# A hybrid decoder layer on one core: transposed sample probabilities taken by matmul with a selection matrix, in place of transposes

## What is computed

```python
def dsa_sample(q, k, v, qi, wi, kidx, cache_k, cache_v, cache_kidx, page_table):
    ...
    sc = jnp.where(causal[None], indexer_scores(qi, wi, kidx_all), -jnp.inf)
    _, idx = lax.top_k(sc, topk)            # 256 of 2056 keys for each new token
    ...
    return sparse_core(q, k_sel, v_sel, valid)

def sparse_core(q, k_sel, v_sel, valid):
    s = jnp.einsum("bthd,btkhd->bthk", q, k_sel, ...) * (DH_ATT ** -0.5)
    s = jnp.where(valid[:, :, None, :], s, -jnp.inf)
    p = jax.nn.softmax(s, axis=-1).astype(v_sel.dtype)
    o = jnp.einsum("bthk,btkhd->bthd", p, v_sel)
```

## Time and profile before

| what | value |
|---|---|
| median of 3 executions | 3352.91 us (3351.32 to 3356.91) |
| the profiled execution: time | 3351.32 us |
| its span | 3349.7 us |
| mean granted TensorE clock | 0.969 of full |
| TensorE busy (matmul records) | 3176.1 us, 95% |
| DVE busy | 1714.9 us, 51% |
| ACT busy | 892.6 us, 27% |
| POOL busy | 667.7 us, 20% |
| HBM traffic over the span | 79 GB/s |

### The profile page before, as it was taken

The page is one execution under the profiler, slowest core; times in us unless marked ns, Lnnn a source line. Parts: engine busy times, 40 slices in busy tenths (PEclk is TensorE's granted clock), DMA queues, the critical chain, the costliest instruction groups (busy, mean ns, idle before and its releaser), DMA issues. The chain is left out here.

```text
span 3349.7 us, 51691 instructions
## 1 busy us (share of the span) xinstructions
PE 3176.1 (95%) x19690; PEld 2928.2 (87%) x19690; DVE 1714.9 (51%) x3021; ACT 892.6 (27%) x1596; POOL 667.7 (20%) x415
## 2 busy tenths in 40 slices
PE   8999999999998999999779898998999999999999
PEld 7999999999998999899545555567999999999999
DVE  6333333334599999996234444444735333333333
ACT  4111111113332332433333333332232111111111
POOL 2212221113433312232320000002121112121111
PEclk9999999999999999999779899998999999999999
DMA  3111111112222223122543436334431111111111
GB/s 111 45 38 50 44 44 44 44 38 68 83 83 76 78 65 88 47 77 85 169 164 114 134 126 195 114 111 138 135 113 38 45 38 50 44 44 44 44 38 67
DMA packets 253375, 265.47 MB, mean 79 GB/s; under 512 B 14527, under 2 KB 193314, under 8 KB 253214
## 3 DMA queue, kind: packets, MB, share of 16 engines
q1 hardware_dynamic: 247738, 254.61, 24.4%
q0 software_dynamic: 4128, 4.20, 0.4%
q10 hardware_dynamic: 1348, 4.49, 0.4%
HBM read 226.20 MB, written 37.05 MB: 79 GB/s over the span
## 5 line engine op out<-in xcount | busy, mean ns | idle before, releaser
L331 PE MATMUL bank<-h_hi,w_hi 128*128 128x362 f32 (+1 forms) x3384 | 1122.8, 332 | 26.1 <-DVE h_lo L218 7.3
L331 PE MATMUL bank<-h_lo,w_hi 128*128 128x362 f32 (+1 forms) x3384 | 1116.4, 330 | 0.0
L331 PE MATMUL bank<-h_hi,w_lo 128*128 128x362 f32 (+1 forms) x3384 | 1112.7, 329 | 0.0
L331 PEld LDWEIGHTS bank<-h_hi,w_hi 128*128 128x128 f32 x3384 | 640.5, 189 | 33.6 <-issue 19.1
L331 PEld LDWEIGHTS bank<-h_lo,w_hi 128*128 128x128 f32 x3384 | 641.1, 189 | 2.8
L331 PEld LDWEIGHTS bank<-h_hi,w_lo 128*128 128x128 f32 x3384 | 642.0, 190 | 0.0
L388 POOL TENSOR_TENSOR w_lo<-raw,w_hi 128x1024 fp32r<-128x1024 f32 x132 | 316.3, 2403 | 1273.1 <-ACT w_hi L483 1273.1
L550 DVE SCALAR_TENSOR_TENSOR x<-bank,x 128x362 f32<-128x362 f32 (+1 forms) x528 | 280.5, 535 | 213.4 <-PE bank L331 213.4
L331 PE MATMUL bank<-a_hi_ffn,w_hi 128*128 128x362 f32 (+1 forms) x1056 | 349.0, 330 | 4.2 <-DVE x L550 2.6
L331 PE MATMUL bank<-a_lo_ffn,w_hi 128*128 128x362 f32 (+1 forms) x1056 | 347.2, 329 | 0.0
L331 PE MATMUL bank<-a_hi_ffn,w_lo 128*128 128x362 f32 (+1 forms) x1056 | 345.8, 327 | 0.0
(11 more groups left out here) (356 smaller groups left out, 4115.9 us busy)
## 6 DMA issues: line engine op xcount, KB each, us to landing
raw<-in_w_ffn_in SPq DMA_DIRECT2D x88, 512.0 KB, 3.8
k_ring<-in_cache_k SPq DMA_DIRECT2D x128, 256.0 KB, 3.8
v_ring<-in_cache_v SPq DMA_DIRECT2D x128, 256.0 KB, 4.0
raw<-in_w_in SPq DMA_DIRECT2D x53, 512.0 KB, 4.9
raw<-in_w_ffn_out SPq DMA_DIRECT2D x44, 512.0 KB, 3.5
kept_g<-stage SPq DMA_DIRECT2D x24, 544.0 KB, 3.1
gate<-kept_g SPq DMA_DIRECT2D x24, 544.0 KB, 3.6
x<-x_kept SPq DMA_DIRECT2D x8, 544.0 KB, 4.6
```

The costliest lines, as they stand in the source:

```text
L331: mm = pe.matmul(out, left, right, start=(start and i == 0 and j == 0), stop=(stop and i == n - 1 and j == 2))
```

## The change

The 17 transposes of a "pt" become 17 matmuls with a selection matrix `own` of 128 x 64 as the moving operand: column n of `own` is the column of the identity that belongs to the n-th good row. The block of `ps` is the stationary operand, so the result is the transposed block with only the 64 good columns, side by side. A bank then holds eight blocks, not four: three turns (8 + 8 blocks, and the tail) take the place of five, and the copies are contiguous. `own` is made by two small copies at the head of DVE's part, and TensorE waits for it (`own_made`). Since a 32-column window for the last tile may no longer reach behind the batch's 64 columns, the tile j = 3 takes columns 32 to 63: its good rows are then the last 16 of its 32, and "ot" copies them apart (four copies, not two). The 16 pad columns of `rep`, `pts` and `qbd` go, and with them two clears.

```diff
-        [("pt", 0), ("pt", 1), ("pt", 2), ("pt", 3), ("pt", 4)],
+        [("pt", 0), ("pt", 1), ("pt", 2)],
...
-            if g < 4:
-                copy(pts[:, 4 * g * NS:(4 * g + 4) * NS].rearrange("p (g j c) -> p g j c", g=4, j=4),
-                     b.rearrange("p (g j c) -> p g j c", g=4, j=4)[:, :, :, 0:16]).then_inc(evicted[me], 1)
+            if g < 2:
+                copy(pts[:, 8 * g:8 * g + 8, :], b.rearrange("p (g n) -> p g n", n=NS)).then_inc(evicted[me], 1)
             else:
-                eng.wait_ge(tail_clear, 1)
...
+                copy(pts[0:DEC_T, PAGES, :], b[0:DEC_T, 0:NS]).then_inc(evicted[me], 1)
...
-                src = b[r, 0:P].rearrange("p (j c) -> p j c", c=32)[:, :, 8 * e:8 * e + DEC_T]
-                ins = copy(qT[r, :, at:at + 8], src)
+                src = b[r, 0:96].rearrange("p (j c) -> p j c", c=32)[:, :, 8 * e:8 * e + DEC_T]
+                copy(qT[r, 0:3, at:at + 8], src)
+                ins = copy(qT[r, 3, at:at + 8], b[r, 112 + 8 * e:120 + 8 * e])
...
-                        a = b * NS + 16 * j
-                        pe.matmul(bank[5][32 * j:32 * j + 32, 0:w], rep[:, a:a + 32],
+                        a = min(16 * j, 32)
+                        pe.matmul(bank[5][32 * j:32 * j + 32, 0:w], rep[:, b, a:a + 32],
...
+                    pe.wait_ge(own_made, 1)
                     pe.wait_ge(s_scaled, s + 1)
                     g = entry[2]
-                    if g < 4:
-                        for q in range(4):
-                            k = 4 * g + q
-                            mm = pe.transpose(tb[:, q * P:(q + 1) * P], ps[:, k * P:(k + 1) * P], ident[:, :])
+                    if g < 2:
+                        for q in range(8):
+                            k = 8 * g + q
+                            mm = pe.matmul(tb[:, q * NS:(q + 1) * NS], ps[:, k * P:(k + 1) * P], own[:, :],
+                                           start=True, stop=True)
                     else:
-                        mm = pe.transpose(tb[0:DEC_T, 0:P], ps[:, PAST:PAST + DEC_T], ident[:, :])
+                        mm = pe.matmul(tb[0:DEC_T, 0:NS], ps[:, PAST:PAST + DEC_T], own[:, :], start=True, stop=True)
...
-            dve.memset(pts[:, PAGES * NS:(PAGES + 1) * NS + 16], 0.0).then_inc(tail_clear, 1)
+            dve.tensor_copy(own[:, 0:48].rearrange("p (j c) -> p j c", c=16),
+                            ident[:, 0:96].rearrange("p (j c) -> p j c", c=32)[:, :, 0:16])
+            dve.tensor_copy(own[:, 48:NS], ident[:, 112:P]).then_inc(own_made, 1)
```

More of the change, by code:

```diff
@@ L598, in decoder_step @@
         bias_s = mem.at("bias_s", [NS, PAST + DEC_T], BF16, AT_B + 9216)
-        rep = mem.at("rep", [NS, DEC_B * NS + 16], BF16, AT_B + 9216 + 4128)
+        rep = mem.at("rep", [NS, DEC_B, NS], BF16, AT_B + 9216 + 4128)
         def dram(name, shape):
@@ L1896, in on_dve @@
             after(dve.tensor_scalar(dst, scores, BARRED * 1.25, BIG, ALU.is_gt, ALU.mult))
-        dve.memset(rep[:, DEC_B * NS:DEC_B * NS + 16], 0.0)
         for b in range(DEC_B):
-            dve.tensor_scalar(rep[:, b * NS:(b + 1) * NS].rearrange("p (h t) -> p h t", h=H),
+            dve.tensor_scalar(rep[:, b, :].rearrange("p (h t) -> p h t", h=H),
                               t8[0:NS, :].unsqueeze(1).to_broadcast([NS, H, DEC_T]), b8[:, 8 * b:8 * b + 1], None,
@@ L2400, in attention @@
     ps = place("ps", [P, PAST + DEC_T], F32, (PAST + DEC_T) * 4)
-    pts = place("pts", [P, (PAGES + 1) * NS + 16], F32, ((PAGES + 1) * NS + 16) * 4)
-    qbd = place("qbd", [P, DEC_B * 4 * NS + 16], F32, 8192 + 64)
-    qbd4 = qbd[:, 0:DEC_B * 4 * NS].rearrange("p (b j n) -> p b j n", b=DEC_B, j=4)
+    own = place("own", [P, NS], F32, NS * 4)
+    pts = place("pts", [P, PAGES + 1, NS], F32, (PAGES + 1) * NS * 4)
+    qbd = place("qbd", [P, DEC_B, 4, NS], F32, 8192)
     qmbd = place("qmbd", [P, DEC_B, 4, 32], F32, 4096)
@@ L2431, in attention @@
     used5, freed5 = sem("used5"), sem("freed5")
-    s_scaled, tail_clear = sem("s_scaled"), sem("tail_clear")
+    s_scaled, own_made = sem("s_scaled"), sem("own_made")
     s_max, s_exp, s_inv, s_norm = sem("s_max"), sem("s_exp"), sem("s_inv"), sem("s_norm")
@@ L2560, in _ @@
         def _(pool):
-            pool.memset(qbd[:, :], 0.0).then_inc(built0, 1)
+            pool.memset(qbd[:, :, :, :], 0.0).then_inc(built0, 1)
             pool.memset(qmbd[:, :, :, :], 0.0).then_inc(built0, 1)
@@ L2571, in _ @@
                         pool.wait_ge(built, h)
-                    pool.tensor_copy(qbd4[r, :, j, h * 8:h * 8 + 8],
+                    pool.tensor_copy(qbd[r, :, j, h * 8:h * 8 + 8],
                                      qT[r, j, SEQ:NT].rearrange("p (b t) -> p b t", b=DEC_B)).then_inc(built, 1)
@@ L2654, in _ @@
                     for j in range(4):
-                        a = b * NS + 16 * j
-                        pe.matmul(bank[5][32 * j:32 * j + 32, 0:w], rep[:, a:a + 32],
+                        a = min(16 * j, 32)
+                        pe.matmul(bank[5][32 * j:32 * j + 32, 0:w], rep[:, b, a:a + 32],
                                   bias_s[:, g * 512:g * 512 + w], start=True, stop=False, tile_position=(0, 32 * j))
                     for j in range(4):
-                        a = (4 * b + j) * NS + 16 * j
+                        a = min(16 * j, 32)
                         keys = kt4[:, g % 2, j, :] if g < 4 else kT[:, j, SEQ + 8 * b:SEQ + 8 * b + 8]
-                        mm = pe.matmul(bank[5][32 * j:32 * j + 32, 0:w], qbd[:, a:a + 32], keys, start=False,
+                        mm = pe.matmul(bank[5][32 * j:32 * j + 32, 0:w], qbd[:, b, j, a:a + 32], keys, start=False,
                                        stop=True, tile_position=(0, 32 * j))
@@ L2683, in _ @@
                     pe.wait_ge(freed5, use_of[entry])
-                    for g in range(5):
+                    for g in range(3):
                         wait_turn(pe, turn_of[("pt", s, g)])
-                    if s == 0:
-                        pe.wait_ge(tail_clear, 1)
                     pe.wait_ge(v_in[0], 128 * (s + 1))
@@ L2694, in _ @@
                         for j in range(4):
-                            a = k * NS + 16 * j
-                            left, right = (pts[:, a:a + 32], v_ring[:, k, j * P:(j + 1) * P]) if k < PAGES else \
-                                (pts[0:DEC_T, a:a + 32], vn[:, j * P:(j + 1) * P])
+                            a = min(16 * j, 32)
+                            left, right = (pts[:, k, a:a + 32], v_ring[:, k, j * P:(j + 1) * P]) if k < PAGES else \
+                                (pts[0:DEC_T, k, a:a + 32], vn[:, j * P:(j + 1) * P])
                             mm = pe.matmul(bank[5][32 * j:32 * j + 32, 0:P], left, right, start=(k == 0),
@@ L2745, in _ @@
                     if b >= 1:
-                        act.wait_ge(turned, turn_of[("pt", b - 1, 4)] + 1)
+                        act.wait_ge(turned, turn_of[("pt", b - 1, 2)] + 1)
                     act.copy(ps[:, g * 512:g * 512 + w], bank[5][:, 0:w]).then_inc(freed5, 1)
```

2 lines of the change are left out of this document (removed).

## The result

The changed kernel took 3373.29 us (median of 4 executions, 3367.89 to 3377.69) against 3353.3 before; the ratio is 1.0057 with a 95% interval of 1.004 to 1.0076. It is slower, as forecast, and by more: 20 us where the sum was +11, and 2.3 us above the range (3363 stated, 3355 to 3371). In two later comparisons, on two chips, the ratio was 1.0041 (1.0027 to 1.0054) and 1.0046 (1.0033 to 1.0058), and the means differ by 14.0 and 14.1 us. Over all 17 executions of the changed kernel and 94 of the kernel before the means are 3368.1 and 3352.0 us, a difference of 16.1 ± 1.2; a single execution of either scatters by about 4.5 us (standard deviation). So 4 to 6 of the first 20 us did not come again.

The account below looks back on a forecast made before the run. TensorE, busy 497.0 of the attention stage's 560.7 us, was taken as the bound. +11.3 us from the "pt" matmuls and 0 from the other parts, on 3351.32, gave 3362.6, stated as 3363, range 3355 to 3371.

Parts of the forecast that it names:

- Part 1, the path: TensorE's "pt" entries: transposes become two-record matmuls, 3.83 us an entry at full clock against 2.50; +11.3 us in all.
- Parts 2, 3, 4 at nothing: Fewer, wider "pt" evictions, four "ot" copies, and layout, clears and `own`: each taken as 0 us.
- The k pages move with the delay: DMA queue in the attention stage: pages shift with TensorE's delay, so its waits for them take none of it back.
- the clock's term of the sum: The "pt" entry of b = 2, starting in a half-clock stretch: +2.0 us, or +4.3 if half clock lasts throughout.
- half clock in more places: Rival, attention stage: later work moves and the clock falls elsewhere too; two more stretches give 3371 us; 10 in 100.
- the moving columns: Rival, "pt" entries: moving columns set the pace, 2.34 us an entry, 2.2 us less, 3349 us; 5 in 100.
- the path did not hide the entries: Rival, attention stage: longer entries only fill TensorE's gaps elsewhere, giving 3351 to 3356 us; 6 in 100.
- the clock did not come back: Rival, attention stage: dense matmuls end all five half-clock stretches, 21.4 us back, giving 3341 us; 5 in 100.

Follow-up runs that it names:

- e8: Kernel before with the change's layout, `own` and four "ot" copies, "pt" left in five turns of transposes: +4.9 ± 1.7 us against the kernel before.
- e2: Kernel before with each of the 16 wide transposes of a "pt" entry issued twice: +11.1 ± 1.9 us against the kernel before.
- e6: Changed kernel, three turns kept, with one transpose for each wide "pt" matmul (other numbers result): -4.3 ± 2.0 us against the kernel before.
- e9: Changed kernel with "pt" as transposes by a 128x128 permutation, good columns first: median 3347.8 us, ratio 0.9987 to the kernel before.
- e11: Changed kernel with two transposes for each "pt" matmul (other numbers result), timed beside the changed kernel: +15.7 ± 1.9 us against the kernel before.
- e12: Changed kernel with `ps` and `own` in one-pass fp32r and each "pt" matmul issued twice: +25.4 ± 2.8 us against the kernel before.
- e3: Kernel before, five turns kept, with "pt" transposes issued as plain f32 matmuls with the identity: +14.6 ± 2.5 us against the kernel before.
- e5: Changed kernel with two transposes for each "pt" matmul (other numbers result), on an earlier occasion: +8.6 ± 1.8 us against the kernel before.

## Why the prediction was right in sign and too low

- *Part 1, the path*: right to 0.1 us an entry at full clock. Two records for each plain f32 matmul, 0.112 us a record, 3.82 to 3.93 us at full clock. The work term at full clock is 31.0 - 20.0 = +11.0.
- *Parts 2, 3, 4 at nothing*: no wait of TensorE appeared for the wide copies, for "ot" or for `own`. e8, though, which is parts 3 and 4 without the new "pt", came out at +4.9 ± 1.7, at a lower clock, so "nothing" holds for the work and was not shown for the time.
- *The k pages move with the delay*: so it was. TensorE's waits for them are 22.4 us, 21.8 before. Aligned step by step, the steps of the stage that run at full clock in both profiles and hold no "pt" differ by 1.3 us in sum when a step is marked by DVE's max over scores, and by -0.1 when it is marked by ACT's exp.
- *The step that failed* is the clock's term of the sum: "The one of b = 2 starts at 1905.00 in a stretch at half clock". One execution's half clock was taken as the place of it, and its amount elsewhere as unchanged, so that half clock entered the sum only in the +2.0 us of the entry of b = 2; "half clock in more places" was a rival at 10 in 100. In fact both place and amount differ from one execution to the next. Of the changed kernel the entry of b = 0 was hit in two of three profiles, at 3.3 us, and that of b = 2 in none. The four executions of the first comparison have a mean clock of 0.967, which is h = 223 us against 205 over all executions before; the later 12 have 0.9691.
- *What half clock costs* can be read in two ways, and they disagree. Between programs: a line through the mean times less entries of the kernels before and changed and of e2 to e6, e8, e9, e11 and e12, against their mean h, has a slope of 0.55 us for each us of half clock when weighted by executions (0.52 when not); the programs lie within 1.3 us of it, e11 within 2.3. Within programs: the executions of one and the same kernel on one chip, 231 in all, have a slope of 0.33 ± 0.02. So the estimate for the first comparison is 11.0 for the entries and 6 to 10 for 18 us more of h, together 17 to 21 of the 20 measured. Over all executions h is 205 us before and 212 changed: 11.0 + 2.1 to 3.6, and 1.5 to 3.0 left of 16.1 ± 1.2. The two later comparisons, at +3.7 and +2.5 us of h, leave about 1 to 2 us of their 14.0 and 14.1, about as large as their errors of 1.7 and 1.6.
- *The range* was built from the bounds of the record and reached up to 3371; with a scatter of 4.5 us for one execution, of which three had been seen, a median of four can lie 2 to 4 us off by itself. 3373.3 was outside.
- *The rivals*: the moving columns did not set the pace, the path did not hide the entries, the clock did not come back. No run here shows that plain matmuls keep the clock better than transposes: with matmuls the mean clock is 0.9690, 0.9692 and 0.9687, with transposes 0.9675 to 0.9702. The Trainium skill, TensorE: Matmul & The Clock Gate, section Part 4: PE-mode transpose, says that a transpose does not count as busy in the same way; these figures do not bear it out.
- *The other page of the Trainium skill*, Perfetto Trace Analysis, section Transposes, says to issue a logical transpose as a transpose. e3 and e9 agree: 12.3 us of entries are lost by the plain matmul alone, and with the selection done by a transpose the entries take 16.1 us where the changed kernel's take 31.0.

What stays open: why one program's mean clock differs between occasions by 0.0026 (e5 and e11), why the two with the one-pass type are lowest (0.9677 and 0.9653), and whether the 0.0008 ± 0.0004 between the kernels before and changed is caused by the change at all; without the first comparison it is 0.0003.

## What to carry to other kernels

Before a transpose is replaced by a matmul that also selects, count the records on TensorE: with 128 stationary columns each took 0.11 us here, whether 64 or 128 columns moved, and plain f32 leaves two where a transpose leaves one; a selection that is wanted anyway can ride on a transpose whose moving operand is a permutation. When a kernel's TensorE has thin places, one profile tells the work but not the time: compare mean clocks over many executions, and take the cost of half clock from them. Turns that stand close together can hide each other's copies; spreading them may put the same copy in front of its consumer.

## Not expected of the hardware

- The granted clock falls to half in places that partly move from one execution to the next; 11 us of useless matmuls ahead of 14 waits raised the mean clock from 0.9692 to 0.9719, and the kernel was 4.3 ± 1.7 us faster with them.
- With 128 stationary columns a plain f32 record takes 0.112 us at 64 and at 128 moving columns alike; with 8 stationary columns it takes 0.060 and 0.112.
- A transpose with a permutation in place of the identity works and costs the same 0.11 us, and transposes may overwrite each other's unwanted half of a bank without a wait.
